# Spreading the norm weights before the filling products, in a one-layer hybrid decoder step

## The chip, the core and the metric

The kernel runs on one core of one Trainium2 chip. The metric is the device time of one execution in microseconds; lower is better. Before the change it is 1681.88 us, the median of three runs (1680.07 to 1683.41).

## What is computed

One layer of a decoder is applied to 1024 prompt tokens and to 8 x 8 sample tokens, 1088 rows of 1024 features, all in float32. Only the first lines concern the change:

```python
def rmsnorm(x, g):
    xf = x.astype(jnp.float32)
    y = xf * lax.rsqrt(jnp.mean(xf * xf, axis=-1, keepdims=True) + EPS)
    return (y * g.astype(jnp.float32)).astype(x.dtype)

def layer(x, conv_prefix, kv_bufs, rel_bias, w_in, ...):
    xn = rmsnorm(x, norm_mix)
    proj = xn @ w_in
    q, k, v, cb, cc, ch, ga, gb = jnp.split(proj, [...], axis=-1)
    ...
```

Behind it come dilated windowed attention over three groups of heads, a gated convolution, the sigmoid gates, the output projection, and an MLP `relu(h @ w_ff1)^2 @ w_ff2` with a final norm.

## The kernel before

Every engine runs a list of instructions written out by hand; semaphores tie the lists together. The tokens lie in nine tiles of up to 128 rows (`xt`, tile 8 has the 64 sample rows). For the first product x must be normalized, turned so that features lie on the partitions, and split in two parts, `xhi` (rounded) and `xlo` (the rest); a block of weights is split the same way into `wh` and `wl`. Each block of 128 output columns (a `Step`) is made in three chunks of 352 or 368 tokens; per chunk TensorE does 8 x 3 products (L647 `xhi,wh`; L648 `xlo,wh`; L649 `xhi,wl`).

**The loads (SyncE).** SP issues tile 0 of x (L384), then the identity matrix (L388, 64 KB), then the norm weights (L389: 4 KB, one row, into partition 0 of `gb`), then tiles 1 and 2, the first block of weights (L380), tiles 3 to 5, the second block, tiles 6 to 8, and small tables. A later block of weights is asked for when its buffer's low part has been made.

**The norm weights.** They are needed on all 128 partitions. TensorE multiplies a row of ones (`sr`, set by GpSimd at the start) with the row `gb`: two products, 512 columns each, into banks 0 and 1 (L727; `gb_pe` counts them). ScalarE copies the first half back to `gb` (L1169) and VectorE the second (L1588); `gb_c` counts the copies, and VectorE's first `scale_x` waits for both.

**The tiles of x.** ScalarE sums the squares of a tile (`square_x`, L1138: an activation and a read of the accumulator). VectorE and ScalarE make the inverse root for tiles 0, 1 to 2, 3 to 5 and 6 to 8 (`rstd_x(n)` L1563 to L1556, `root_x(n)` L1143). VectorE scales a tile by that and by `gb` in one operation (`scale_x`, L1568). TensorE turns it in eight transposes, four to a bank (`turn_x`, L695), ScalarE takes `xhi` out of the bank in two pieces (L1150) and VectorE `xlo` (L1578). In between ScalarE makes `wh` (L1124) and VectorE `wl` (L1540). VectorE's order at the start is

```python
        rstd_x(0)
        dve.wait_ge(gb_pe, 2)
        dve.tensor_copy(gb[:, 512:D], bank[1][:]).then_inc(gb_c, 1)
        dve.wait_ge(gb_c, 2)
        scale_x(0)
        rstd_x(1)
        scale_x(1)
        split_x_lo(0)
        scale_x(2)
        split_x_lo(1)
        split_lo(Step(0), KD)
        split_x_lo(2)
        rstd_x(2)
        scale_x(3)
```

**TensorE at the start.** It waits for the identity, issues 28 filling products (`keep_warm`, L720: identity times identity, 128 columns, into bank 7, which nobody reads), then waits for the norm weights and the ones, spreads the weights, issues two more fills, and turns tiles 0, 1 and 2 with two fills behind each. It waits for six pieces of `xlo` (three tiles) and begins the first chunk; the turns of tiles 3 to 8 stand between halves of chunks (`chunk_turning`). From then on products follow one another to the end of the kernel.

Of the kernel before, what the change touches and what calls it, by code (L numbers as in the profile page):

```python
# [57 lines left out]
CH = ((0, 352), (352, 368), (720, 368))  # L58
TABLE = 384

WARM = (28, 2)
DIAG0 = 255
CH_LAST = ((0, 384), (384, 384), (768, 320))
FIRST, FIRST_TILES = 768, 6
# [87 lines left out]
def build(nc, x_p, x_s, ckv, state, w_in, w_att, w_conv, w_o, conv_w, conv_b, rel_bias, g_mix,  # L152
# [479 lines left out]
    def _(pe):  # L632
# [53 lines left out]
        def turn_x(t):  # L686
            w = rows_of(t)
            pe.wait_ge(x_scaled, t + 1)
            for half in range(2):
                n = 2 * t + half  # L690

                if above_zero(n - 3):
                    pe.wait_ge(x_lo, n - 3)
                for k in range(4):
                    last = pe.transpose(bank[3 + n % 4][:, k * P:k * P + w],  # L695
                                        xt[0:w, t, (4 * half + k) * P:(4 * half + k + 1) * P], ident[0:w, 0:w])
                last.then_inc(x_pe, 1)
# [19 lines left out]
        def keep_warm(n):  # L717

            for _ in range(n):
                pe.matmul(bank[7][:, 0:P], ident[:], ident[:], start=True, stop=True)  # L720

        pe.wait_ge(id_in, 16)
        keep_warm(WARM[0])
        pe.wait_ge(gb_in, 16)
        pe.wait_ge(ones_row, 1)
        for half in range(2):
            pe.matmul(bank[half][:], sr[:, 0, :], gb[0:1, 512 * half:512 * half + 512], start=True, stop=True).then_inc(gb_pe, 1)  # L727
        keep_warm(WARM[1])
        for t in range(3):
            turn_x(t)  # L730
            keep_warm(WARM[1])
        pe.wait_ge(x_lo, 6)
# [384 lines left out]
    def _(act):  # L1117
# [15 lines left out]
        def square_x(t):  # L1133
            w = rows_of(t)
            act.wait_ge(x_in[t], 16)
            if t:
                act.wait_ge(x_sq, t)
            act.activation(junk[0:w, :], xt[0:w, t, :], ACT.Square, accum_out=ssq[0:w, t:t + 1]).then_inc(x_sq, 1)  # L1138

        def root_x(n):  # L1140
            act.wait_ge(rs_d, 5 * n + 1)
            cut = slice(*NORM_TILES[n])
            act.activation(rst[:, 1, cut], rst[:, 0, cut], ACT.Sqrt).then_inc(rs_a, 1)  # L1143
# [21 lines left out]

        square_x(0)
        root_x(0)
        act.wait_ge(gb_pe, 2)
        act.activation(gb[:, 0:512], bank[0][:], ACT.Copy).then_inc(gb_c, 1)  # L1169
        square_x(1)  # L1170
        square_x(2)
        root_x(1)
        split_x_hi(0)
# [1008 lines left out]
```

## Time and profile before

| | |
|---|---|
| median of three runs | 1681.88 us |
| profiled execution, time | 1683.65 us |
| profiled execution, first to last instruction (span) | 1681.9 us |
| mean granted TensorE clock over the span | 0.996 |
| TensorE matmul busy | 1647.1 us (98%) |
| VectorE busy | 687.9 us (41%) |
| ScalarE busy | 483.2 us (29%) |
| start of the first fill / of the spreading products / of the first real product | 4.46 / 13.62 / 27.04 us |

All starts are counted from the first instruction of the span. A granted clock of 1.00 is 2.4 GHz and 0.50 is 1.2 GHz. Each float32 product is two entries in the trace. An entry's time can overlap the next one's, so the distance between starts, not an entry's length, tells the rate.

### The profile page before, as it was taken

Reading aid. Unit: us, or ns where it says so; the run is one execution under the profiler, and the core shown is the slowest. Engines: PE = TensorE matmul, PEld = TensorE weight load, DVE = VectorE, ACT = ScalarE, POOL = GpSimd, SP = SyncE. Lnnn points to the kernel's source line nnn. Section 1 sums busy time; section 2 is a strip of 40 time slices with the busy share of each in tenths; the row PEclk is TensorE's granted clock in tenths of the full one; section 3 lists DMA queues with packets and bytes.
Section 4 is the critical chain, followed back from the end, with each engine's and each line's share of the span. In section 5 each row is a group of like instructions: output and inputs, shape, how many; then the busy total and the mean of one; then the engine's idle time right before and its main releaser. Section 6 shows DMA issues by size and latency. Waiting matters only on the chain. (4 is left out here: it accounts for less than half of the span.)

```text
span 1681.9 us, 28428 instructions
## 1 busy us (share of the span) xinstructions
PE 1647.1 (98%) x10711; PEld 1596.5 (95%) x10711; DVE 687.9 (41%) x1236; ACT 483.2 (29%) x925; POOL 79.1 (5%) x94
## 2 busy tenths in 40 slices
PE   7999999999989999999999999999999999999997
PEld 7899999888988999999999999999999999999997
DVE  5212223334644444333654353333333333333566
ACT  5222224433534443111423320133111320133223
POOL 0160000000000000000121000000000000000021
PEclk9999999999999999999999999999999999999999
DMA  5254554332257785532111112111111111111224
GB/s 163 83 154 130 163 172 137 103 106 95 85 153 178 190 200 148 168 110 84 51 38 50 50 30 58 37 50 37 50 41 46 41 46 50 37 50 37 63 67 153
DMA packets 237202, 155.87 MB, mean 93 GB/s; under 512 B 23982, under 2 KB 227590, under 8 KB 237146
## 3 DMA queue, kind: packets, MB, share of 16 engines
q1 hardware_dynamic: 208590, 124.00, 26.2%
q10 hardware_dynamic: 26268, 28.31, 5.0%
q0 software_dynamic: 2288, 2.80, 0.7%
q8 instruction: 37, 0.61, 0.1%
q14 instruction: 19, 0.16, 0.0%
HBM read 122.00 MB, written 35.43 MB: 94 GB/s over the span
## 5 line engine op out<-in xcount | busy, mean ns | idle before, releaser
L647 PE MATMUL bank<-xhi,wh 128*128 128x352 f32 (+1 forms) x1104 | 372.0, 337 | 3.9 <-DVE xlo L1578 1.8
L648 PE MATMUL bank<-xlo,wh 128*128 128x352 f32 (+1 forms) x1104 | 360.2, 326 | 0.0
L649 PE MATMUL bank<-xhi,wl 128*128 128x352 f32 (+1 forms) x1104 | 359.8, 326 | 0.0
L1124 ACT ACTIVATE wh<-wr 128x1024 fp32r<-128x1024 f32 (+1 forms) x142 | 144.6, 1018 | 433.0 <-PE bank L649 332.0
L1540 DVE TENSOR_TENSOR wl<-wr,wh 128x1024 fp32r<-128x1024 f32 (+1 forms) x142 | 181.6, 1279 | 188.7 <-ACT wh L1124 187.5
L648 PE MATMUL bank<-hlo,wh 128*128 128x368 f32 (+1 forms) x768 | 251.4, 327 | 0.0
L647 PE MATMUL bank<-hhi,wh 128*128 128x368 f32 (+1 forms) x768 | 250.6, 326 | 0.3 <-DVE rel L1964 0.3
L649 PE MATMUL bank<-hhi,wl 128*128 128x368 f32 (+1 forms) x768 | 250.1, 326 | 0.0
L647 PEld LDWEIGHTS bank<-xhi,wh 128*128 128x128 f32 x1104 | 207.3, 188 | 15.5 <-issue 7.6
L648 PEld LDWEIGHTS bank<-xlo,wh 128*128 128x128 f32 x1104 | 207.6, 188 | 0.0
L649 PEld LDWEIGHTS bank<-xhi,wl 128*128 128x128 f32 x1104 | 207.5, 188 | 0.0
L648 PE MATMUL bank<-flo,wh 128*128 128x368 f32 (+1 forms) x576 | 188.8, 328 | 0.0
L647 PE MATMUL bank<-fhi,wh 128*128 128x368 f32 (+1 forms) x576 | 187.9, 326 | 0.0
L649 PE MATMUL bank<-fhi,wl 128*128 128x368 f32 (+1 forms) x576 | 187.6, 326 | 0.0
L647 PEld LDWEIGHTS bank<-hhi,wh 128*128 128x128 f32 x768 | 144.1, 188 | 0.6 <-issue 0.6
L649 PEld LDWEIGHTS bank<-hhi,wl 128*128 128x128 f32 x768 | 144.6, 188 | 0.0
L648 PEld LDWEIGHTS bank<-hlo,wh 128*128 128x128 f32 x768 | 144.2, 188 | 0.0
L1964 DVE TENSOR_TENSOR rel<-bank,rel 128x368 f32<-128x368 f32 (+1 forms) x96 | 51.5, 536 | 150.7 <-ACT rel L1472 150.7
L649 PEld LDWEIGHTS bank<-fhi,wl 128*128 128x128 f32 x576 | 108.5, 188 | 0.0
L648 PEld LDWEIGHTS bank<-flo,wh 128*128 128x128 f32 x576 | 108.1, 188 | 0.1
L647 PEld LDWEIGHTS bank<-fhi,wh 128*128 128x128 f32 x576 | 108.0, 188 | 0.1
L1977 DVE TENSOR_TENSOR acc<-bank,r2b 128x368 f32<-128x368 f32 (+1 forms) x72 | 38.6, 536 | 157.0 <-PE bank L649 157.0
(235 smaller groups left out, 2069.1 us busy)
## 6 DMA issues: line engine op xcount, KB each, us to landing
wr<-in_w_ff_dram SPq DMA_DIRECT2D x72, 512.0 KB, 3.9
wr<-in_w_in_dram SPq DMA_DIRECT2D x46, 512.0 KB, 4.2
d_T<-stg ACTq DMA_DIRECT2D x18, 544.0 KB, 2.8
kvc<-in_cache_kv_g_dram SPq DMA_DIRECT2D x16, 512.0 KB, 6.1
kvc<-in_cache_kv_g_dram SPq DMA_DIRECT2D x32, 256.0 KB, 7.3
d_tm<-tm ACTq DMA_DIRECT2D x12, 512.0 KB, 3.7
d_m<-bb ACTq DMA_DIRECT2D x8, 544.0 KB, 3.1
ml<-d_m SPq DMA_DIRECT2D x8, 544.0 KB, 4.4
```

The costliest lines, as they stand in the source:

```text
L647: pe.matmul(bank[c][:, 0:n], wh[st_.p][:, k, :], a, start=(k == 0), stop=False)
L648: pe.matmul(bank[c][:, 0:n], wh[st_.p][:, k, :], b, start=False, stop=False)
L649: last = pe.matmul(bank[c][:, 0:n], wl[st_.p][:, k, :], a, start=False, stop=(k == nk - 1))
L1124: act.activation(wh[st_.p][:, 0:nk, :], wr[st_.p][:, 0:nk, :], ACT.Copy).then_inc(w_hi, 1)
L1540: dve.tensor_tensor(wl[st_.p][:, 0:nk, :], wr[st_.p][:, 0:nk, :], f32(wh[st_.p][:, 0:nk, :]), ALU.subtract).then_inc(w_lo, 1)
L1964: dve.tensor_tensor(r[:, 0:n], bank[c][:, 0:n], r[:, 0:n], ALU.mult).then_inc(taken[c], 1)
L1977: dve.tensor_tensor(acc[:, 0:n], bank[c][:, 0:n], r2b[:, t0:t0 + n], ALU.mult).then_inc(taken[c], 1)
```

## The change

TensorE's wait for the norm weights and the two spreading products come first, right behind the wait for the identity. The 28 fills ahead of them and the 2 behind them go; 8 fills stand behind them. On ScalarE the copy of the first half of `gb` moves from in front of the square of tile 1 to behind it. Nothing else differs.

```diff
-WARM = (28, 2)
+WARM = (8, 2)
...
         pe.wait_ge(id_in, 16)
-        keep_warm(WARM[0])
         pe.wait_ge(gb_in, 16)
         pe.wait_ge(ones_row, 1)
         for half in range(2):
             pe.matmul(bank[half][:], sr[:, 0, :], gb[0:1, 512 * half:512 * half + 512], start=True, stop=True).then_inc(gb_pe, 1)
-        keep_warm(WARM[1])
+        keep_warm(WARM[0])
         for t in range(3):
             turn_x(t)
             keep_warm(WARM[1])
...
         square_x(0)
         root_x(0)
+        square_x(1)
         act.wait_ge(gb_pe, 2)
         act.activation(gb[:, 0:512], bank[0][:], ACT.Copy).then_inc(gb_c, 1)
-        square_x(1)
         square_x(2)
         root_x(1)
```

## Rows read from the trace of the kernel before

**Rows 1.** The page: busy time, share of the span, instructions.

```profile
PE 1647.1 (98%) x10711; PEld 1596.5 (95%) x10711; DVE 687.9 (41%) x1236; ACT 483.2 (29%) x925; POOL 79.1 (5%) x94
```

**Rows 2.** Waits of TensorE, 0 to 60 us: total, times, longest.

```profile
PE bank L695 <- DVE xt L1568: 3.5, 3, 1.5
PE bank L647 <- DVE xlo L1578: 1.8, 1, 1.8
PE bank L647 <- DVE wl L1540: 0.8, 1, 0.8
```

**Rows 3.** Timeline of TensorE, 3 to 24 us: start, length, what, count.

```profile
4.46 9.24 PE L720 MATMUL bank<-ident 128*128 128x128 f32 x56 [4.46 <-DMA ident<-in_identity_dram]
13.62 1.98 PE L727 MATMUL bank<-gb,sr 1*128 1x512 f32 x4
...
17.78 1.97 PE L695 MATMUL bank<-ident,xt 128*128 128x128 f32 x8 [1.54 <-DVE xt L1568]
```

**Rows 4.** Timeline of TensorE, 26 to 31 us.

```profile
27.04 0.43 PE L647 MATMUL bank<-xhi,wh 128*128 128x352 f32 x1 [1.77 <-DVE xlo L1578]
...
30.64 0.55 PE L695 MATMUL bank<-ident,xt 128*128 128x128 f32 x3 [1.41 <-DVE xt L1568]
```

**Rows 5.** Timeline of ScalarE, 0 to 27 us.

```profile
4.23 1.06 ACT L1138 ACTIVATE junk<-xt 128x1024 f32<-128x1024 f32 x1 [1.98 <-DMA xt<-in_x_prompt_dram]
5.19 0.19 ACT L1138 ACTIVATION_READ_ACCUMULATOR junk<-xt 128x1 f32 x1
...
15.64 0.60 ACT L1169 ACTIVATE gb<-bank 128x512 f32<-128x512 f32 x1 [9.84 <-PE bank L727]
...
18.93 0.60 ACT L1150 ACTIVATE xhi<-bank 128x512 fp32r<-128x512 f32 x1
19.79 0.60 ACT L1150 ACTIVATE xhi<-bank 128x512 fp32r<-128x512 f32 x1 [0.26 <-PE bank L695]
```

**Rows 6.** Timeline of VectorE, 13 to 27 us.

```profile
15.72 0.69 DVE L1588 COPY gb<-bank 128x512 f32<-128x512 f32 x1 [9.14 <-PE bank L727]
16.44 1.28 DVE L1568 SCALAR_TENSOR_TENSOR xt<-xt,rst,gb 128x1024 f32<-128x1024 f32 x1
18.55 0.17 DVE L1563 TENSOR_SCALAR rst<-ssq 128x2 f32<-128x2 f32 x1 [0.82 <-ACT junk L1138]
...
19.78 1.28 DVE L1568 SCALAR_TENSOR_TENSOR xt<-xt,rst,gb 128x1024 f32<-128x1024 f32 x1
```

**Rows 7.** DMA packets, 3.3:4.15 and 4.15:4.95; issues; landings of tiles 1, 2, 8.

```profile
DMA packets 205, 0.25 MB, mean 289 GB/s; under 512 B 33, under 2 KB 161, under 8 KB 205
...
DMA packets 52, 0.21 MB, mean 266 GB/s; under 512 B 0, under 2 KB 0, under 8 KB 52
...
2.05 0.83 SPq L384 DMA_DIRECT2D xt<-in_x_prompt_dram x2
...
11.55 0.57 SPq L386 DMA_DIRECT2D xt<-in_x_sample_dram x1
...
DMA to landing us min/median/max: 5.3/5.3/5.3
...
DMA to landing us min/median/max: 6.3/6.3/6.3
...
DMA to landing us min/median/max: 9.4/9.4/9.4
```

**Rows 8.** Windows: busy time (x entries) of PE, PEld, DVE, ACT, POOL; clock; DMA.

```profile
17.10:23.80 6.70, 5.50 (x25) 5.21 (x26) 5.47 (x11) 4.92 (x11) 0.00 (x0) 0.50 0.28 51
24.00:26.00 2.00, 1.28 (x12) 1.08 (x10) 2.00 (x4) 2.00 (x5) 0.00 (x0) 1.00 0.00 0
...
30.64:54.00 23.36, 23.30 (x156) 22.50 (x156) 15.62 (x25) 9.13 (x19) 0.00 (x0) 1.00 0.08 23
```

**Rows 9.** Fill passes begun 4.5 to 9.7 and 10.6 to 13.4 us: ns min/median/max.

```profile
L720 PE MATMUL bank<-ident x25: 421/421/579, 4.5 to 9.7; 128*128 128x128 f32 x25
...
L720 PE MATMUL bank<-ident x26: 275/275/275, 10.6 to 13.4; 128*128 128x128 f32 x26
```

## The prediction

> **What bounds the kernel now.** I read first the page's list of busy times: TensorE holds 98% of the span [rows 1], so from the moment its long run of products begins, everything is a shift of that run. The whole effect of this edit must therefore come from when the run begins, and from its clock there. Second, the waits of TensorE in the first 60 us [rows 2]: besides the opening wait for the identity it stands 3.5 us for scaled tiles (`DVE xt L1568`) and 1.8 us for the low half of the third tile (`DVE xlo L1578`). Neither wait names the spread weights, so third I read the timeline of TensorE [rows 3, 4] and of the two engines that work on x [rows 5, 6], to see what those waits hang on. The fills begin at 4.46 and last 9.24 us (56 passes for 28 fills, so two passes each); only then, at 13.62, come the spreading products, 1.98 us. ScalarE has been idle for 9.84 us and VectorE for 9.14 us when they copy the result [rows 5, 6]. VectorE scales tile 0 at 16.44 and then goes on nearly without a pause until the last `xlo` of tile 2, which ends TensorE's wait of 1.77 us before the first real product at 27.04 [rows 4]. After that TensorE pauses once more, 1.41 us, until tile 3 is scaled, and goes on at 30.64 [rows 4]. From there to 54 us it is busy 23.30 of 23.36 us [rows 8]. So the point to shift is 30.64, and what sets it is a chain: weights spread, tile 0 scaled, squares and scales of tiles 1 to 5 on ScalarE and VectorE.
>
> **What comes out and what moves.** 28 + 2 fills around the products become 8 behind them: 22 fills, 44 passes, are gone. None of them feeds anything, so their own time is not the saving; the saving is that the products no longer stand behind them. The products need the identity wait (passed at 4.46), the ones (a GpSimd memory set at the very start) and the 4 KB of norm weights.
>
> *When do the norm weights land?* The trace gives no landing for that transfer. It is issued right behind the identity on SP's queue. In the DMA view of 3.3 to 4.15 us there are 33 packets under 512 B, and none from 4.15 to 4.95 [rows 7]. Tile 0 and the identity raise a semaphore by 16 each; if each such packet is one of these marks, 33 is 16 + 16 + 1, the one being the single row of weights. The Trainium skill, page "DMA: Bandwidth & Descriptors", section "Why a DMA increments its semaphore by 16 and not by 1", states that only the engines a transfer uses post such a mark, one each; the trace's 33 agrees with it. The other bound from rows is 13.62, where the products found the weights there. I take 4.5, for the identity, issued just ahead, released the fills at 4.46.
>
> *The products at the lower clock.* At 13.62 they ran fast: 26 fill passes begin between 10.6 and 13.4, 0.112 us apart, against 25 between 4.5 and 9.7, 0.217 us apart [rows 9]. That ratio is 1.94. The four passes of the products, 1.98 us, therefore take about 1.98 x 1.94 = 3.8 us in the new place; the bounds are 1.98 and 3.8, and the stretch is exactly the one where the fills ran slowly, so 3.8. They end at 4.5 + 3.8 = 8.3.
>
> *ScalarE.* Its square of tile 1 now precedes its copy. Tiles 1 and 2 are issued between 2.05 and 2.88, tile 1 first; it lands at 2.05 + 5.3 = 7.35 [rows 7]. Tile 0's square and its read took from 4.23 to 5.38, 1.15 us [rows 5], so this one runs to 8.5; the copy (0.60) then runs 8.5 to 9.1. VectorE's copy (0.69, starting 0.1 after the products) runs 8.4 to 9.1 [rows 6]. Moving the copy behind the square thus costs about 0.2 us on ScalarE, and almost nothing at the meeting of the two. Tile 0 is scaled from 9.15 in place of 16.44: 7.3 us earlier.
>
> *A second small gain.* Before, VectorE stood 0.82 us before the root of tiles 1 and 2, waiting for ScalarE's second square [rows 6]. Now one square is already behind, and the other (tile 2, issued near 2.45, landed 6.3 later, at 8.8 [rows 7]) runs 9.1 to 10.3, while tile 0 is scaled until 10.44. The 0.82 goes: the scale of tile 1 starts 19.78 - 18.55 = 1.23 us after that, at 11.65, which is 8.1 earlier.
>
> *What takes some of it back.* The 8 fills stand before the turning of tile 0. They start when the products are through, or a little ahead, since entries overlap: 8.1 to 8.3. 16 passes x 0.217 = 3.5 put the turn at 11.6, where tile 0 has been ready since 10.5. The first `xhi` follows a slow turn by 1.15 us (18.93 against 17.78) and the second by 2.0 (19.79) [rows 3, 5], so the second is done at 14.2; VectorE can finish the `xlo` of tile 0 at 14.9. Before, that was done about 2 x 1.28 after 19.78, at 22.3: 7.4 earlier. If the clock stays low, the two slow turns and four slow fills that follow hold the later `xhi`: third turn at 16.8, its second `xhi` 18.8 to 19.4, last `xlo` done 20.1, first product 20.15, 6.9 earlier. ScalarE's squares of tiles 4 and 5 then end at 21.7, and the scale of tile 3 (1.25 us of root, 1.28) at 24.3: 30.64 comes 6.3 earlier. If the clock rises by the second turn, VectorE alone bounds: with some 1.2 to 1.28 for each large step [rows 6] it is through the scale of tile 2 at 16.1, `xlo` of tile 1 at 17.3, the low weights at 18.5, `xlo` of tile 2 at 19.6; first product 19.7, 7.3 earlier; ScalarE is through square 5 at 20.1, the scale of tile 3 is done at 22.7, and 30.64 comes 7.9 earlier. From 8.1 to about 17 TensorE has hardly a pause in the new order (fills, turn, fills, turn, with 1.2 us between two VectorE steps), while before it fell to the half clock during products and an idle stretch, 17.1 to 23.8 [rows 8]. I take the middle: 7.0.
>
> *Transfers.* The loads of x keep their times; they are now nearer to their use. The last, the sample rows, land 11.55 + 9.4 = 20.9 [rows 7]; ScalarE reaches them behind the root of tiles 3 to 5 (21 or later) and the squares of tiles 6 and 7, so after 23. Two us of cover are left at least. The third block of input weights is asked for when the first low weights are made, 7 us earlier, and is needed only after the six chunks of the first two blocks, which fill the window to 54 [rows 8]; its cover stays as it was.
>
> **Sum.** Products 7.3 earlier, plus 0.8 on VectorE's wait, less 1.0 at the fills and slow turns (0.2 to 1.8): 7.0, between 6.3 and 7.9. The profiled execution took 1683.65 (span 1681.9 and 1.75 around it); minus 7.0 that is 1676.65. Its time lies 1.8 above the median shown, so against the median: 1681.88 - 7.0 = 1674.9.
>
> **Rivals.**
> (a) *The run starts at the half clock.* The clock was 0.50 from 17.1 to 23.8, after the stretch of one-partition products and a pause, and full from 24 on, although TensorE rested 1.77 and 1.41 us there [rows 4, 8]. In the new order it rests some 2 us before the first product. If it falls there for as long as before (6.7 us), the run loses half of that, 3.4, less 0.9 that its own pause at tile 3 absorbs: 7.9 - 2.5 = 5.4 gained, down to about 4.5 where turns were slow too: 1676.5 to 1677.4. Against it: rests of nearly that length did no harm. The Trainium skill, page "TensorE: Matmul & The Clock Gate", section "Part 4: PE-mode transpose", says that transposes do not count as busy time for the full clock. By that rule the turns keep nothing warm once 22 fills are gone, which is this rival; the trace neither bears it out nor refutes it, since two fills stand behind each turn before the clock came up.
> (b) *The weights land late*, say with tile 1 at 7.35, not at 4.5. Then the products end near 11.2, tile 0 is scaled near 12.0, 4.4 earlier: 1677.4. The 33 packets speak against it.
> (c) *No change.* The gain is lost at a later wait for something that did not move, a transfer or GpSimd's tables. It would need a pause of 7 us in the cover; the one wait for weights in the first 60 us (0.8, low weights [rows 2]) is for VectorE, which shifts along. 1681.9.
> (d) *Slower.* The clock does not come up again with the run: at the half clock every 2 us of work lose 1. It decides against the change from about 2 x (7.9 + 0.9) = 18 us at half clock after the first product, and costs 0.2% from about 25 us, giving 1685.3. The longest such stretch shown is 6.7 us, so this is remote.
>
> **Chances and range.** Forecast 0.64, (a) 0.14, (b) 0.06, (c) 0.12, (d) 0.04. 0.2% is 3.4 us, about what a measurement of this kernel can tell from no change (the three runs lie 3.3 us apart). The first three cases are faster by more: 0.84; (c) is 0.12; (d) 0.04. The likeliest case's own range is 1674.0 to 1675.6 by the sum. With about 1.3 us of scatter of a median below, and (a) and (b) with 1.1 above, the range is 1672.7 to 1678.5; it leaves out (c) and (d).
>
> **What would show it.** The products of `L727` start at about 4.5 with four passes over some 3.8 us; if they start near 7.4 or later, (b). Both copies of `gb` end near 9.1. `xt L1568` starts at 9.15 and again at 11.65, without the 0.8 us wait for `junk L1138`. TensorE's first turn starts behind the fills at about 11.6. The first `L647` stands at 19.7 to 20.2 at full clock; at 0.5 there, (a). The row at 30.64 comes at 22.7 to 24.3, and what follows keeps that shift to the end; a new wait of several us between 24 and the end would be (c). I am wrong most if the clock behaves otherwise than its one rise and fall here suggest.

## The result and the profile after

The changed kernel takes 1674.56 us, the median of five runs (1673.81 to 1675.57); the kernel before takes 1681.88 (1680.07 to 1683.53). The ratio is 0.9954, 95% interval 0.9943 to 0.9965: 7.3 us faster, 7.0 were forecast, and the whole interval lies beyond the 0.2% that the prediction asks for. The profiled execution took 1675.57 against 1683.65, 8.1 us less.

The timeline of TensorE after the change, 3 to 24 us, answers to [rows 3, 4]:

```profile
4.49 3.78 PE L726 MATMUL bank<-gb,sr 1*128 1x512 f32 x4 [4.49 <-DMA ident<-in_identity_dram]
8.20 3.78 PE L720 MATMUL bank<-ident 128*128 128x128 f32 x16
11.77 1.07 PE L695 MATMUL bank<-ident,xt 128*128 128x128 f32 x8
...
15.62 1.09 PE L695 MATMUL bank<-ident,xt 128*128 128x128 f32 x8 [1.00 <-DVE xt L1567]
16.55 0.61 PE L720 MATMUL bank<-ident 128*128 128x128 f32 x4
19.14 0.43 PE L647 MATMUL bank<-xhi,wh 128*128 128x352 f32 x1 [1.99 <-DVE xlo L1577]
...
22.36 1.09 PE L695 MATMUL bank<-ident,xt 128*128 128x128 f32 x8 [1.02 <-DVE xt L1567]
```

The four product passes start at 4.49, released by the identity, and last 3.78 us, as long as the 16 fill passes behind them; the first turn is already fast (1.07 us for what took 1.97). The first real product stands at 19.14 in place of 27.04, the turn of tile 3 at 22.36 in place of 30.64: 7.9 and 8.3 us earlier.

VectorE's timeline after answers to [rows 6]:

```profile
8.38 0.69 DVE L1587 COPY gb<-bank 128x512 f32<-128x512 f32 x1 [1.74 <-PE bank L726]
9.11 1.28 DVE L1567 SCALAR_TENSOR_TENSOR xt<-xt,rst,gb 128x1024 f32<-128x1024 f32 x1
10.31 0.16 DVE L1562 TENSOR_SCALAR rst<-ssq 128x2 f32<-128x2 f32 x1
...
11.53 1.28 DVE L1567 SCALAR_TENSOR_TENSOR xt<-xt,rst,gb 128x1024 f32<-128x1024 f32 x1
13.08 1.29 DVE L1577 TENSOR_TENSOR xlo<-bank,xhi 128x512 fp32r<-128x512 f32 x2 [0.27 <-ACT xhi L1149]
```

Its wait for the products fell from 9.14 to 1.74 us, the wait of 0.82 before the second root is gone, and a new one of 0.27 stands before the first `xlo`: the fills delay the turn of tile 0, and that is all VectorE feels of it at this point.

### The profile page after: what moved, and what is told of

Its sections match the earlier page's. It is cut to its first block and busy times, and to the rows that moved or that the text cites. A ratio compares the mean times of both kernels' runs of the same rounds, so it can differ in the third digit from the quotient of the medians.

```text
span 1673.8 us, 28340 instructions
## 1 busy us (share of the span) xinstructions
PE 1640.2 (98%) x10667; PEld 1588.5 (95%) x10667; DVE 687.7 (41%) x1236; ACT 482.6 (29%) x925; POOL 79.1 (5%) x94
## 5 line engine op out<-in xcount | busy, mean ns | idle before, releaser
L648 PE MATMUL bank<-hlo,wh 128*128 128x368 f32 (+1 forms) x768 | 251.4, 327 | 0.0
```

Source lines behind the costliest of these rows:

```text
L648: pe.matmul(bank[c][:, 0:n], wh[st_.p][:, k, :], b, start=False, stop=False)
```

## The experiments

Every time stands beside runs of the kernel before on the same chip; a ratio below 1 is faster. Since single runs scatter by 2 to 4 us, "turn 3" gives the start of the turn of tile 3 in each profile (30.64 before): what the beginning gains is read there without the rest of the kernel.

| kernel | median us | before us | ratio [95% interval] | turn 3 |
|---|---|---|---|---|
| the change | 1674.56 | 1681.88 | 0.9954 [0.9943, 0.9965] | 22.36 |
| 1 eight fills in front | 1676.10 | 1682.44 | 0.9965 [0.9951, 0.9978] | 26.10 |
| 2 twenty-eight behind | 1679.60 | 1682.44 | 0.9981 [0.9972, 0.9990] | 26.99 |
| 3 none behind | 1673.04 | 1682.44 | 0.9943 [0.9930, 0.9957] | 22.43 |
| 4 ScalarE's part alone | 1681.18 | 1682.44 | 0.9994 [0.9985, 1.0003] | 29.56 |
| 5 the change again | 1674.43 | 1681.36 | 0.9957 [0.9944, 0.9971] | 22.26 |
| 6 none behind again | 1671.81 | 1681.36 | 0.9942 [0.9928, 0.9955] | 22.31 |
| 7 copy before square | 1674.23 | 1681.36 | 0.9953 [0.9939, 0.9966] | 22.78 |
| 8 ScalarE reordered | 1671.24 | 1681.36 | 0.9938 [0.9925, 0.9952] | 21.20 |
| 9 no fill at all | 1673.70 | 1682.56 | 0.9951 [0.9938, 0.9965] | 22.82 |
| 10 fills on one partition | 1687.37 | 1682.56 | 1.0026 [1.0014, 1.0037] | 34.81 |
| 11 twenty small more | 1675.68 | 1682.37 | 0.9964 [0.9951, 0.9978] | 22.18 |
| 12 none, eight small | 1675.38 | 1682.37 | 0.9959 [0.9945, 0.9972] | 21.79 |

### 1. Fewer fills, but in front

```diff
         pe.wait_ge(id_in, 16)
+        keep_warm(WARM[0])
         pe.wait_ge(gb_in, 16)
...
-        keep_warm(WARM[0])
+        keep_warm(WARM[1])
```

> The changed kernel with its 8 fills put back in front of the spreading products and 2 behind them: as few fills as in the change, in the order of before. Theory (the order is what pays: the copies of gb wait for the products, and the products for what stands ahead of them): 16 slow passes of 0.217 take 3.5 us, so tile 0 is scaled near 12.5 in place of 9.1 and the time is 3.4 us above the change's 1674.6, about 1678.0. Rival (dropping fills is what pays, wherever they stand): about 1674.6, as the change.

TensorE's timeline of this run:

```profile
4.36 3.78 PE L720 MATMUL bank<-ident 128*128 128x128 f32 x16 [4.36 <-DMA ident<-in_identity_dram]
8.07 3.78 PE L727 MATMUL bank<-gb,sr 1*128 1x512 f32 x4
11.78 1.22 PE L720 MATMUL bank<-ident 128*128 128x128 f32 x4
14.03 1.97 PE L695 MATMUL bank<-ident,xt 128*128 128x128 f32 x8 [1.03 <-DVE xt L1568]
```

Tile 0 is scaled at 12.69 and the turn of tile 3 stands at 26.10: 4.5 us of the 8.3 remain, 3.7 are lost to sixteen passes ahead of the products. So the order is what pays at the beginning, beyond having fewer fills. The time itself was 1676.1, lower than the 1678.0 forecast, and by medians alone (0.9965 against 0.9954, overlapping intervals) the two would not be told apart; the starts tell them apart. Not all of the 3.7 us reach the end of these two profiles: by the starts of the same products 2.4 are left at 900 us and 1.1 at the end. Part goes at a wait of TensorE for VectorE near 516 us, which takes 1.69 us in the change and 0.93 in run 1, and 1.3 go near 1650 us, where the clock falls for 3.4 us in the change and not in run 1 (see the last section). The wait near 516 us differs between executions of one and the same kernel: 1.69 in the change, 0.56 in run 5, which is the change again:

```profile
516.92 0.19 PE L913 MATMUL bank<-ident,sr 1*128 1x1 f32 x1 [1.69 <-DVE sr L1862]
```

```profile
515.49 0.19 PE L913 MATMUL bank<-ident,sr 1*128 1x1 f32 x1 [0.56 <-DVE sr L1862]
```

### 2. All fills, but behind

```diff
-WARM = (8, 2)
+WARM = (28, 2)
```

> The changed order with all 28 fills, now behind the spreading products. Theory (fills behind cost too, once they outlast the scale of tile 0 at 10.4): the fills end near 16.2 in place of 11.8, the first turn is 4.4 us later and nothing recovers it; about 1679.0. Rival (only what stands ahead of the products costs): about 1674.6.

The fills run from 8.41 to 16.6, VectorE has scaled tile 1 long before, and then waits 4.68 us for `xhi`. Turn 3 is at 26.99, 4.6 later than in the change, as the theory has it, and the time 1679.6. Fills cost where something waits behind them, on either side of the products. In this run TensorE's opening wait reads so:

```profile
PE bank L726 <- DMA gb<-in_norm_mix_dram: 4.7, 1, 4.7
```

The weights landed at 4.73: after the identity, but by only some 0.2 to 0.3 us.

### 3 and 6. No fill behind the products, and the change beside it

```diff
-WARM = (8, 2)
+WARM = (0, 2)
```

> The changed order with no fill behind the spreading products (the two behind each turn stay). Theory (the 8 fills delay the first turn by 1.3 us, of which VectorE feels about 0.3, but they bring the clock up before the turns): first turn near 10.5 at half clock, the first product near 19 with the clock not yet up, and up to 2.5 us lost in the first chunk; 1674.6 to 1677. Rival (fills do nothing for the time): the clock comes up all the same, first product near 18.9, about 1674.3.

> The changed kernel once more, to stand beside the next two on the same chip. About 1674.6. The scatter of single runs (1673.8 to 1675.6 so far) is the measure for the others.

> The changed order with no fill behind the products, again. In its first profile the turn of tile 3 stood at 22.43 against 22.36 in the changed kernel, so the beginning gives no reason for the 1.5 us by which its median was lower. Theory (that difference came from later in the kernel and is scatter): within 1 us of the changed kernel run beside it. Rival (the fills cost 1.5 us somewhere): 1.5 us faster again.

TensorE's timeline of the first run without them:

```profile
4.40 3.78 PE L726 MATMUL bank<-gb,sr 1*128 1x512 f32 x4 [4.40 <-DMA ident<-in_identity_dram]
10.36 1.97 PE L695 MATMUL bank<-ident,xt 128*128 128x128 f32 x8 [2.18 <-DVE xt L1567]
12.12 1.06 PE L720 MATMUL bank<-ident 128*128 128x128 f32 x4
```

The first turn comes 1.4 us earlier but runs slowly, and the beginning ends where it did: turn 3 at 22.43 and 22.31, against 22.36 and 22.26 with the eight fills. For the beginning they do neither good nor harm. The theory of the first run was wrong there: the clock was up before the first real product (18.70), whose successors start 0.16 us apart, the pace of full clock, so nothing was lost in the first chunk. But both times the whole kernel was faster, by 2.6 us in the set where both ran together (1671.81 against 1674.43; the ratios' intervals overlap, so the size is not firm). My theory of mere scatter did not explain it. The two traces of each pair keep step until about 264 us and then part by 1.3 to 1.4 us within ten; runs 11 and 12 are about that place. In the profiles of runs 5 and 6 another 1.5 us come near 1650 us, where the clock falls in run 5 and not in run 6: that part is no merit of the kernel.

### 4. ScalarE's move alone

```diff
         square_x(0)
         root_x(0)
+        square_x(1)
         act.wait_ge(gb_pe, 2)
         act.activation(gb[:, 0:512], bank[0][:], ACT.Copy).then_inc(gb_c, 1)
-        square_x(1)
```

> The kernel before with the move on ScalarE alone: the square of tile 1 ahead of the copy of gb. Theory: the square runs in ScalarE's idle time before 15.6, VectorE's wait of 0.82 us before the second root goes, 0.8 us faster than before, 1681.1. Rival (that wait is made up for later by another, so the move gives nothing): 1681.9.

VectorE's 0.82 us are gone (the second root starts at 17.32, the end of the scale). Turn 3 is 1.08 earlier, of which 0.32 came before the products (they began at 13.30), so 0.76 is the move's. In the time it is -0.06%, interval -0.15% to +0.03%: not measurable.

### 7. The change without ScalarE's move

```diff
         root_x(0)
-        square_x(1)
         act.wait_ge(gb_pe, 2)
         act.activation(gb[:, 0:512], bank[0][:], ACT.Copy).then_inc(gb_c, 1)
+        square_x(1)
```

> The changed kernel with ScalarE's order of before: the copy of gb ahead of the square of tile 1. Theory: the products end at 8.3, the copy runs to 8.9, VectorE's own copy to 9.1, so tile 0 is scaled at 9.1 all the same; but two squares (2.3 us) now stand behind the copy, until 11.3 in place of 9.9, and VectorE waits about 0.9 us before the second root, as it did before; first product 0.6 to 0.9 later, about 1675.3. Rival (the order on ScalarE decides when gb is ready): first scale earlier or later by the square, 1.2 us.

VectorE's timeline here:

```profile
9.04 1.28 DVE L1567 SCALAR_TENSOR_TENSOR xt<-xt,rst,gb 128x1024 f32<-128x1024 f32 x1
11.15 0.17 DVE L1562 TENSOR_SCALAR rst<-ssq 128x2 f32<-128x2 f32 x1 [0.82 <-ACT junk L1137]
```

Tile 0 is scaled at the same moment (9.04 against 9.11) and the old wait of 0.82 is back. Turn 3 is 0.4 to 0.5 later, the time equal within its scatter. So nearly all the gain is TensorE's order; ScalarE's move is worth about half a microsecond here, 0.76 in run 4.

### 8. The last pause before the gapless run

```diff
-        split_x_hi(0)
         split_hi(Step(0), KD)
-        split_x_hi(1)
+        split_x_hi(0)
         square_x(3)
-        split_x_hi(2)
+        split_x_hi(1)
         square_x(4)
+        split_x_hi(2)
         square_x(5)
```

(without the fills behind the products)

> No fill behind the products, and on ScalarE the high weights made before the first xhi and the squares of tiles 3 and 4 moved one place ahead each. Theory (the turn of tile 3, the last pause before the gapless run, hangs on ScalarE's square of tile 5, which ends at 19.8): that square ends near 18.9, the turn of tile 3 comes near 21.5 in place of 22.4, 1 us faster than the run without fills beside it. Rival (VectorE or TensorE bounds there): no difference.

The square of tile 5 ends at 18.29 (19.74 in the change) and turn 3 stands at 21.20, where TensorE rests 0.25 us in place of 1.52. That is 1.1 earlier than in run 6 beside it. The median, 1671.24, is the lowest of all, 0.6 under run 6; the intervals overlap (ratios 0.9938 and 0.9942), so against run 6 it is shown in the trace alone. It beats the kernel before clearly; against the change beside it (run 5) its median is 3.2 us lower, but the ends of the two intervals still touch.

### 9. No fill at all

```diff
-WARM = (8, 2)
+WARM = (0, 0)
```

> The changed order with no fill at all, neither behind the products nor behind the turns of tiles 0 to 2. Theory (fills are what brings the clock up before the first real product): the first product stands near 18.9 at half clock, and the first chunk and the next turns lose 1 to 2.5 us; 1675 to 1677. Rival (the turns alone suffice, or the loss hides in the pauses): as without the 8 fills, about 1673.5 to 1674.5.

Windows of this run (length, busy time of TensorE, its weight loads, VectorE, ScalarE, GpSimd, granted clock, DMA), and the first real product:

```profile
18.84:22.80 3.96, 3.89 (x12) 3.44 (x12) 2.16 (x7) 3.54 (x9) 0.00 (x0) 1.00 0.65 150
...
18.84 0.66 PE L647 MATMUL bank<-xhi,wh 128*128 128x352 f32 x1 [1.56 <-DVE xlo L1577]
```

The twelve products of the first half chunk (one entry each, where a fill or a spreading product is two) take until 22.8 in place of some 2.2 us: they run at the half clock. The column says 1.00 all the same, because the records begin with the first rise, at 22.9 here; ahead of it the clock is read from the distance between passes. Yet turn 3 is only 0.4 later than without the eight fills (22.82 against 22.43), since TensorE would have waited there for tile 3 anyway. So the theory was right on the start at the half clock and wrong on its price: 1673.70, in the range that the rival gave. Rival (a) of the prediction priced such a start at 2.5 us.

### 10. Fills on one partition

```diff
+        pe.wait_ge(ones_row, 1)
-        keep_warm(WARM[0])
+        for _ in range(WARM[0]):
+            pe.matmul(bank[7][:, 0:P], sr[:, 0, :], sr[:, 0, :], start=True, stop=True)
         pe.wait_ge(gb_in, 16)
-        pe.wait_ge(ones_row, 1)
```

(in the kernel before)

> The kernel before, with its 28 leading fills on one partition: ones times ones, 128 columns, so as many passes of the same length, but only one of 128 rows. Theory (one-partition products leave the clock at its half level; the spreading products show no rise): 56 passes of 0.213 are 12.0 us in place of 9.2, the spreading products take 3.8 in place of 2.0, and the first real product comes 4.6 us later; about 1686.5. Rival (they count like any product): the clock comes up near 10 us as before, 1681.9.

```profile
4.43 12.31 PE L725 MATMUL bank<-sr 1*128 1x128 f32 x56 [4.43 <-DMA ident<-in_identity_dram]
16.54 3.62 PE L728 MATMUL bank<-gb,sr 1*128 1x512 f32 x4
20.09 1.22 PE L720 MATMUL bank<-ident 128*128 128x128 f32 x4
```

Almost sixteen microseconds of unbroken one-partition products left the clock at its half level: 56 passes take 12.3 us (0.22 each) and the spreading products 3.6. With full fills it had risen near 10 us [rows 9]. Turn 3 is 4.2 us late, the time 0.26% up, as forecast. So nothing here suggests that the spreading products, moved to the front, help to bring the clock up. One thing beside the number of partitions differs from the fills: both operands were all ones. No run separates the two.

### 11 and 12. What happens near 264 us

ScalarE's timeline there, the change:

```profile
263.31 0.39 ACTq L1209 DMA_DIRECT2D d_tm<-tm  x1
263.85 0.61 ACTq L1210 DMA_DIRECT2D d_tm<-tm  x1
264.56 2.12 ACTq L1215 DMA_DIRECT2D out_dram<-tm  x1
266.76 1.27 ACTq L1225 DMA_DIRECT2D out_dram<-tm  x2
```

and without the fills behind (run 3):

```profile
264.77 0.70 ACTq L1215 DMA_DIRECT2D out_dram<-tm  x1
265.56 1.27 ACTq L1225 DMA_DIRECT2D out_dram<-tm  x2
```

One issue takes 2.12 us in place of 0.70. ScalarE's exponentials of the first attention scores come later by that, and TensorE waits for VectorE at 275:

```profile
275.16 1.13 PE L771 MATMUL bank<-kT,qT 64*128 64x256 f32 x8 [1.50 <-DVE st L1668]
```

The DMA view of the change, 264.40 to 264.56, has a packet of the instruction queue; in run 3 the same view finds it at 266.5 to 266.6:

```profile
DMA packets 95, 0.06 MB, mean 365 GB/s; under 512 B 12, under 2 KB 94, under 8 KB 94
...
q8 instruction: 1, 0.02, 71.7%
```

It is a fetch of code (16 KB), and it comes later the fewer products TensorE has issued before. To move it alone, I added small products where TensorE rests:

```diff
         for t in range(3):
             turn_x(t)
             keep_warm(WARM[1])
+            for _ in range(10 if t else 0):
+                pe.matmul(bank[7][0:8, 0:8], sr[:, 0, 0:8], sr[:, 0, 0:8], start=True, stop=True)
```

> The changed kernel with 20 small products more (one partition, 8 columns, into the unread bank), 10 behind the turns of tiles 1 and 2 each, where TensorE rests anyway 1 and 2 us. Nothing waits for them. In the profiles so far, a 16 KB packet of the instruction queue falls within 0.1 us of one store's issue on ScalarE near 264 us in all four runs of kernels with 14 to 16 fills, and that issue takes 1.9 to 2.1 us; with 0, 6, 34 or 36 fills the packet is 1.7 us or more away and the issue takes 0.6 to 0.9. Theory (the number of TensorE's instructions sets when the packet comes, and the meeting costs 1.2 us): 20 more products make 34, the packet comes some 2 us ahead of the issue, the issue takes 0.7, and the kernel is 1.2 us FASTER than the change although it does more: about 1673.3. Rival (the meeting is chance, or the packet is not TensorE's): as the change, 1674.5, or slower by what the small products take.

> The changed order with no fill behind the products, and 8 small products (one partition, 8 columns), 4 behind the turns of tiles 1 and 2 each, so 14 fills and small ones together, as many as the change has fills. Theory: the packet falls on the issue near 264 us again, the issue takes near 2 us, and the kernel loses the 1.2 us that it had over the change: the beginning as without fills (turn of tile 3 at 22.4), time about 1673.5 against 1672.0 to 1672.4 without the small ones. Rival: 1672.

(The second with 4 in place of 10, and `WARM = (0, 2)`.) ScalarE's issue in the two:

```profile
264.49 0.66 ACTq L1217 DMA_DIRECT2D out_dram<-tm  x1
```

```profile
264.01 1.98 ACTq L1217 DMA_DIRECT2D out_dram<-tm  x1
```

The issue, 0.66 and 1.98 us, does both times what the theory says. Over all fourteen profiles, by the number of fills and small products on TensorE, with the distance of the packet from the issue, and the time from turn 3 to the attention product at 275 us:

| products | kernels | packet to issue, us | issue, us | turn 3 to 275, us |
|---|---|---|---|---|
| 0 | 9 | +4.23 | 0.70 | 251.75 |
| 6 | 3, 6, 8 | +1.75 to +2.54 | 0.68 to 0.70 | 251.5 to 251.8 |
| 14 to 16 | the change, 1, 5, 7, 12 | -0.11 to -0.04 | 1.87 to 2.12 | 252.6 to 253.0 |
| 34 to 36 | before, 2, 4, 10, 11 | -2.26 to -2.22 | 0.64 to 0.70 | 251.4 to 251.7 |

The meeting costs 0.8 to 1.6 us, about 1.2. As forecasts of the whole time, though, the theory failed for both runs. Run 12 took 1675.38 where 1673.5 was forecast; its ratio (0.9959) stands with the change (0.9954, 0.9957) and not with runs 3 and 6 (0.9943, 0.9942), as the meeting would have it, but the intervals overlap. Run 11 took 1675.68, no faster than the change. It gained 1.3 us at 264, and lost as much again at 400, because the next packet now met another store:

```profile
400.51 2.29 ACTq L1351 DMA_DIRECT2D d_st<-stT  x1
```

That issue takes 0.34 us in the change, but 2.30 in the kernel before (at 408.90), and 2.3 to 3.4 in runs 2, 4, 10 and 11: all that have 34 to 36 products. I had looked at one meeting and not at the ones that follow. Nor is a packet beside an issue enough to make it long. In run 5 a 16 KB packet begins 0.13 us ahead of ScalarE's issue at 128.27, which takes 0.35 us, and in run 2 one begins 0.08 us ahead of SyncE's issue at 300.65, which takes 0.38. Where they meet at 264 us the packet itself is slow too, 1.6 to 1.8 us against 0.9 to 1.3 where it comes apart from the issue. That the meeting there costs time is shown by moving it both ways; what sets the price, and why other meetings cost nothing, stays open. The Trainium skill, page "Runtime: NRT & Kernel Launch", section "Instruction fetch mechanics", says that instructions are refilled in blocks of 16 KiB and that crossing a block is mostly hidden; the trace agrees with the size, and shows that the refill need not be hidden from another engine that is issuing a DMA just then.

## Why the prediction was right

**The bound.** That everything hangs on the turn of tile 3 held: 8.3 us gained there, 8.1 in the profiled executions, 7.3 in the medians.

**The products.** Forecast 4.5 to 8.3 and 3.8 us long; measured 4.49 and 3.78. That the weights would be there was right: the reading of the 33 small packets [rows 7] held, and run 2 caught the landing itself at 4.73. Rival (b) fell with it.

**The copies and the scale.** 9.15 forecast, 9.11 measured; the second scale 11.65 against 11.53. The 0.82 went; runs 4 and 7 show that ScalarE's move is what removes it. One step was wrong without harm: tile 1 did not land at 7.35 but at 6.73, so its square was through at 7.9 and the copy waited for the products (8.30), not for the square.

**What takes some back.** This term was mis-sized: 1.0 forecast (0.2 to 1.8), about zero at turn 3. (As written, 7.3 + 0.8 - 1.0 also gives 7.1, not 7.0.) The start of the turns at 11.6 was right (11.77), but I let the clock rise only by the second turn, and it was full at the first. The second `xhi` was therefore done at 13.5, not 14.2. So the first real product came at 19.14, ahead of my 19.7 to 20.2, and turn 3 at 22.36, ahead of my 22.7 to 24.3. The fills did take their toll at first: ScalarE began the first high weights at 13.42 against 20.28, 6.9 us earlier and not 8.3. It was given back because before the change the turn of tile 1 had been slow, and ScalarE had stood 0.94 and 0.26 us waiting for its halves (at 22.27 and 23.12); after the change it does not wait there:

```profile
22.27 0.60 ACT L1150 ACTIVATE xhi<-bank 128x512 fp32r<-128x512 f32 x1 [0.94 <-PE bank L695]
23.12 0.60 ACT L1150 ACTIVATE xhi<-bank 128x512 fp32r<-128x512 f32 x1 [0.26 <-PE bank L695]
```

```profile
14.37 1.09 ACT L1149 ACTIVATE xhi<-bank 128x512 fp32r<-128x512 f32 x2
```

The square of tile 5, on which turn 3 hangs, so ends 8.3 us earlier (19.74 against 28.02). Runs 3 and 6 show besides that a slow first turn costs nothing there, as it may then start 1.4 us earlier.

**The later part.** I took the rest of the kernel to shift as a block. It nearly did in the sum, but by two effects that cancel in part: the change meets a code fetch at 264 us that before did not, and misses the one that before met at 408. Of the 8.28 at turn 3, 6.9 are left at the attention product at 275 (282.06 against 275.16); by 430 us 8.2 are back, and the span ends 8.1 apart. So the profiled executions show 8.1 saved, more than the 7.9 at which the sum ended; the medians show 7.3, and 6.9 in run 5. That these came so near 7.0 is in part luck: the forecast was about 1 us low by the trace, and the scatter between executions is as large.

**The transfers.** "The loads of x keep their times" was not quite so: the sample rows landed 11.1 us after their issue in place of 9.4, at 22.7. In run 5, the same kernel, they took 8.9, with the third weights asked for at 17.82 against 17.92; so this too differs from execution to execution, and an earlier request for the third weights is not what makes it. ScalarE squares them at 24.27; 1.5 us of cover were left, not 2.

**Rival (a).** The first product ran at full clock. Run 9 shows a start at the half clock and what it costs at turn 3: 0.4 us, not 2.5, for the clock came up after 4 us and not after 6.7, and the pause at tile 3 hid the rest. Run 9 also bears on the rule of the Trainium skill on transposes (page "TensorE: Matmul & The Clock Gate", section "Part 4: PE-mode transpose"): with turns alone, 5.8 of 6.7 us busy (10.5 to 17.2), the clock did not rise until after the real products began, which agrees with it; it does not prove it, for TensorE also paused 0.45 and 0.42 us between the turns. Rivals (c) and (d) did not come.

## What to carry to other kernels

Filling work belongs behind what others wait for, and only as far as nothing waits behind it; at turn 3 it cost its full length otherwise, on either side. Count the gain at the last pause before the gapless run, and use the start of one instruction there to compare variants: it told 0.4 us apart where medians could not tell 1.5. It tells what the beginning gains, not what is left of it at the end: of the 3.7 us between the change and run 1 the profiles kept 1.1. And a change in the number of instructions moves the later code fetches; before a microsecond gained or lost "somewhere later" is called scatter, look for a DMA issue that takes 2 us beside a packet of the instruction queue, and compare it with the other profiles: one of ScalarE's issues, between 46 and 59 us, takes 2.2 to 2.6 us in all fourteen and so explains no difference.

## What the runs showed of the hardware

- Products with one row of 128 active, ones times ones, did not raise TensorE's clock: almost 16 us of them without a pause left it at 1.2 GHz (run 10); with full fills it rose near 10 us. In run 1 TensorE was busy from 4.36 to 13.0 without a pause, 3.8 us of it on one-partition products, and the turns that followed were still slow.
- A code fetch of 16 KB that began 0.04 to 0.17 us ahead of one of two DMA issues on ScalarE made that issue take 1.9 to 3.4 us in place of 0.3 to 0.7: at 264 to 269 us in five of the fourteen profiles and at 400 to 413 us in five others. Other issues with such a packet as near stayed short (run 5 at 128.27, run 2 at 300.65).
- Full load does not hold the clock for good: in seven of the fourteen profiles it goes to its half level once for some 3.4 us near 1650 us, with TensorE busy throughout. Runs 2, 7 and 12 have one such fall elsewhere, at 480, 518 and 474 us, and runs 1, 6, 8 and 10 none before the very end. The windows of the kernel before and of run 1:

```profile
1652.00:1655.40 3.40, 3.40 (x16) 3.40 (x14) 2.97 (x4) 1.05 (x2) 1.21 (x1) 0.50 0.94 280
```

```profile
1600.00:1671.00 71.00, 65.15 (x433) 63.31 (x431) 49.65 (x75) 22.94 (x33) 15.27 (x10) 1.00 0.34 108
```

By the starts of the same products, run 1 gains about 1.3 us on the kernel before across that stretch. That is one part of the scatter; what sets the fall off stays open. Between 400 and 530 us the differences come in part from these falls and in part from the wait near 516 us shown under run 1, which takes between 0.4 and 1.9 us in the change and runs 3, 5 and 7; what sets its length was not looked into.
